# Eight modulation tiles computed in the low-rank stage, three instead of four in each iteration of the mixing

## The reference

```python
mod_all = jnp.einsum('bd,lde->lbe', jax.nn.silu(c), ada_w) + ada_b[:, None, :]
...
shift1, scale1, gate1, shift2, scale2, gate2 = jnp.split(mod_all[i], 6, axis=-1)
h = _modulate(x, shift1, scale1)
...
x = x + gate1[:, None, :] * y
h = _modulate(x, shift2, scale2)
x = x + gate2[:, None, :] * _swiglu(h, f_w1[i], f_w3[i], f_w2[i])
```

## Time and profile before

| | us |
|---|---|
| median of three runs | 2634.53 |
| the profiled execution | 2638.5 |
| span of its trace, from the first to the last instruction | 2636.9 |
| low-rank stage, first matmul to first scan of the mixing | 327.9 to 373.5 |
| mixing, first scan to first matmul of `w_o` | 373.5 to 684.6 |
| steady iteration, scan to scan | 34.5 |

### The profile page before, as it was taken

One profiled execution on the slowest core, in us unless ns is written; L12 is line 12 of the kernel. 1 busy time (PEld: TensorE's weight loads), 2 busy tenths in 40 slices (PEclk: granted clock), 3 DMA queues, 4 the chain that ended last, 5 costly groups with the idle time before them and its releaser, 6 DMA issues.

```text
span 2636.9 us, 53505 instructions
## 1 busy us (share of the span) xinstructions
PE 2526.7 (96%) x20124; PEld 2221.2 (84%) x20124; DVE 1898.7 (72%) x2611; ACT 1251.8 (47%) x1926; POOL 46.3 (2%) x85
## 2 busy tenths in 40 slices
PE   7999997888899999999999999999999999999998
PEld 6888877777788888888888888888888888888887
DVE  6868737988687777777777776687887655555556
ACT  2245555666445444444444554344554444444445
POOL 2000020000000000000000000000000000000000
PEclk9999999999999999999999999999999999999999
DMA  9999864556477888888888768566788666665654
GB/s 400 416 319 306 287 228 153 162 165 211 153 259 255 284 288 287 277 285 289 283 284 271 227 221 286 201 231 229 242 291 284 200 189 190 191 192 187 188 165 138
DMA packets 443401, 640.28 MB, mean 243 GB/s; under 512 B 22048, under 2 KB 403104, under 8 KB 422432
## 3 DMA queue, kind: packets, MB, share of 16 engines
q1 hardware_dynamic: 439552, 626.35, 70.6%
q0 software_dynamic: 3744, 12.59, 1.3%
HBM read 624.18 MB, written 14.68 MB: 242 GB/s over the span
## 4 chain that ended last, share of the span: by engine, by line
PE 67%; DVE 5%; ACT 1%; DMA 1%; issue 1%; DVEq 0%; SPq 0%; ACTq 0%
PE ps L1790 43%; PE ps L1794 22%; DVE ada_ring L1836 1%; DVE wlo L1774 1%; DMA ada_ring<-in_ada 1%; ACT whi L1769 1%; DVE nt L132 0%; PE ps L1425 0%; PE ps L1419 0%; DVE act L145 0%; DVE st L1326 0%; PE ps L1458 0%; DVE lgf L1323 0%; PE ps L1450 0%; PE ps L1440 0%
## 5 line engine op out<-in xcount | busy, mean ns | idle before, releaser
L1774 DVE TENSOR_TENSOR wlo<-raw,whi 128x1024 fp32r<-128x1024 f32 (+1 forms) x736 | 865.3, 1191 | 437.6 <-ACT whi L1769 436.5
L1790 PE MATMUL ps<-act,whi 128*128 128x512 f32 x3528 | 1095.5, 392 | 1.0 <-DVE act L145 1.0
L1769 ACT ACTIVATE whi<-raw 128x1024 fp32r<-128x1024 f32 (+1 forms) x736 | 746.0, 1030 | 638.7 <-PE ps L1794 630.9
L1794 PEld LDWEIGHTS ps<-act,wlo 128*128 128x128 f32 x3528 | 662.6, 188 | 146.3
L1794 PE MATMUL ps<-act,wlo 128*128 128x256 f32 x3528 | 696.3, 279 | 0.0
L1790 PE MATMUL ps<-hid,whi 128*128 128x512 f32 x2176 | 685.6, 396 | 8.1 <-DVE wlo L1774 7.0
L1790 PEld LDWEIGHTS ps<-act,whi 128*128 128x128 f32 x3528 | 534.6, 188 | 1.6 <-DVE wlo L1774 1.0
L1794 PEld LDWEIGHTS ps<-hid,wlo 128*128 128x128 f32 x2176 | 411.5, 189 | 92.6
L1794 PE MATMUL ps<-hid,wlo 128*128 128x256 f32 x2176 | 433.2, 279 | 0.0
L1790 PEld LDWEIGHTS ps<-hid,whi 128*128 128x128 f32 x2176 | 330.9, 189 | 10.7 <-DVE wlo L1774 4.4
L1836 DVE SCALAR_TENSOR_TENSOR ada_ring<-ada_ring,silu 128x2048 f32<-128x2048 f32 x128 | 292.4, 2285 | 12.7 <-DMA ada_ring<-in_ada 12.7
(11 more groups left out here) (273 smaller groups left out, 2062.5 us busy)
## 6 DMA issues: line engine op xcount, KB each, us to landing
raw<-in_f_w SPq DMA_DIRECT2D x480, 512.0 KB, 4.6
ada_ring<-in_ada SPq DMA_DIRECT2D x144, 1024.0 KB, 7.6
raw<-in_a_w_rkv SPq DMA_DIRECT2D x96, 512.0 KB, 7.7
ada_ring<-in_ada SPq DMA_DIRECT2D x64, 512.0 KB, 4.5
raw<-in_b_w_in SPq DMA_DIRECT2D x56, 512.0 KB, 4.2
raw<-in_f_w SPq DMA_DIRECT2D x64, 384.0 KB, 3.9
first_ring<-in_ada SPq DMA_DIRECT2D x16, 1024.0 KB, 12.7
raw<-in_a_w_o SPq DMA_DIRECT2D x32, 512.0 KB, 7.5
```

Of the source, the lines that this page charges most:

```text
L1769: self.nc.scalar.activation(self.whi[:, u % SPL, 0:n], self.raw[:, u, 0:n], ACT.Copy).then_inc(self.s("hi_ready"), 1)
L1774: self.nc.vector.tensor_tensor(self.wlo[:, u % SPL, 0:n], self.raw[:, u, 0:n], self.whi[:, u % SPL, 0:n].bitcast(F32), SUB).then_inc(self. ...
L1790: self.nc.tensor.matmul(self.ps[0:c1 - c0, banks[b], :], hi[:, kk, c0:c1], src[:, k].rearrange("p a t -> p (a t)"), start=k == 0, stop=False)
L1794: last = self.nc.tensor.matmul(self.ps[0:c1 - c0, banks[b], T:2 * T], lo[:, kk, c0:c1], src[:, k, 0, :], start=False, stop=k == ktotal - 1)
```

## The change

Tiles 48 to 55 are computed in the low-rank stage, in a ring of three places of a whole tile (`lora_ring`), in memory that is not used in that stage. The mixing does the other 24 tiles: three in each iteration, six halves, in three of the four places of `ada_ring`.

```diff
-ADA_FIRST = 48
+ADA_LORA, ADA_FIRST = 48, 56
...
     def sync(self, sp):                      # class Loras
         p, s = self.p, self.p.s
+        sp.wait_ge(s("unit_used"), self.units)
+
+        def rows(n):
+            if n > 2:
+                sp.wait_ge(s("ada_added"), ADA_LORA + n - 2)
+            sp.dma_start(p.lora_ring[n % 3][:], p.ada_rows(ADA_LORA + n)).then_inc(s(f"lora_rows{n % 3}"), 16)
+        for n in range(3):
+            rows(n)
         for u in range(RAW):
             sp.wait_ge(s("native_used"), self.n0 + u + 1)
             p.load_unit(sp, u, self.outer(u))
+            if 2 <= u <= 6:
+                rows(u + 1)
...
     def vector(self, dve):                   # class Loras
         for k in range(KT):
-            self.mixed.dve_one(dve, 4, self.p.lmix[1], k, k, k)
+            self.mixed.dve_one(dve, 4, p.lmix[1], k, k, k)
+        for n in range(ADA_FIRST - ADA_LORA):
+            dve.wait_ge(s(f"lora_rows{n % 3}"), 16 * (n // 3 + 1))
+            tile = p.lora_ring[n % 3][:]
+            p.nc.vector.scalar_tensor_tensor(tile, tile, 1.0, p.silu[:], MUL, MUL,
+                                             accum_out=p.mod[:, ADA_LORA + n:ADA_LORA + n + 1]).then_inc(s("ada_added"), 1)
+        at = slice(ADA_LORA, ADA_FIRST)
+        dve.wait_ge(s("ada_added"), ADA_FIRST)
+        p.nc.vector.tensor_tensor(p.mod[:, at], p.mod[:, at], p.pv[:, PV_ADA + ADA_LORA:PV_ADA + ADA_FIRST], ADD).then_inc(s("lora_mods"), 1)
...
-        TILES = 2 * KT // L
+        TILES = (2 * KT - (ADA_FIRST - ADA_LORA)) // L
...
         def place(n):
-            return self.ada_ring[:, n // 2 % 2, (n % 2) * W:(n % 2 + 1) * W]
+            m = n % 3
+            return self.ada_ring[:, m // 2, (m % 2) * W:(m % 2 + 1) * W]
...
-                    if not (isinstance(i, int) and i == 0 and n < 4):
-                        sp.wait_ge(s("ada_half"), i * HALVES + (n - 3))
+                    if not (isinstance(i, int) and i == 0 and n < 3):
+                        sp.wait_ge(s("ada_half"), i * HALVES + (n - 2))
...
             def body(i, more):
-                ada(i, 6, 7)
-                ada(i + 1, 0, 1, 2, 3)
+                ada(i, 4, 5)
+                ada(i + 1, 0, 1, 2)
                 if more:
                     tiles(i + 2)
                 gates(i)
-                ada(i + 1, 4, 5)
+                ada(i + 1, 3)
...
-            ada(0, 0, 1, 2, 3)
+            ada(0, 0, 1, 2)
             tiles(1)
             loras.gates_stored(sp)
-            ada(0, 4, 5)
+            ada(0, 3)
...
-            ada(L - 1, 6, 7)
+            ada(L - 1, 4, 5)
             gates(L - 1)
...
-                adas(i, 5, 6)
+                adas(i, 5)
                 grow(i, "W32", 1, SUB, "P4")
                 if prep:
                     prep_c(i + 1, 1 - q)
-                adas(i, 7)
                 grow(i, "W64", 3, SUB, "W32")
```

More of the change, by code:

```diff
@@ L796, in vector @@
     def vector(self, dve):
-        dve.wait_ge(self.p.s("unit_used"), self.units)
+        p, s = self.p, self.p.s
+        dve.wait_ge(s("unit_used"), self.units)
         for k in range(KT):
-            self.mixed.dve_one(dve, 4, self.p.lmix[1], k, k, k)
+            self.mixed.dve_one(dve, 4, p.lmix[1], k, k, k)
[7 more added lines that the diff above has]
+        p.nc.vector.tensor_tensor(p.mod[:, at], p.mod[:, at], p.pv[:, PV_ADA + ADA_LORA:PV_ADA + ADA_FIRST], ADD).then_inc(s("lora_mods"), 1)
     def pool(self, pool):
@@ L1698, in layout @@
                 b[n] = rw(f"{n}{j}", [P, NC, 2, HD])
+            if j == 0:
+                self.lora_ring = [v("lora_ring0", [P, D], o[0])]
+            else:
+                self.lora_ring += [v(f"lora_ring{n}", [P, D], o_u + 4 * D * (n - 3)) for n in (1, 2)]
             b["bon"] = [rw(f"bon{q}_{j}", [P, T]) for q in range(2)]
@@ L1954, in place @@
         def place(n):
-            return self.ada_ring[:, n // 2 % 2, (n % 2) * W:(n % 2 + 1) * W]
+            m = n % 3
+            return self.ada_ring[:, m // 2, (m % 2) * W:(m % 2 + 1) * W]
         def ada_half(dve, i, n):
-            dve.wait_ge(s(f"half_loaded{n % 4}"), i * 32 + 16 * (n // 4 + 1))
+            dve.wait_ge(s(f"half_loaded{n % 3}"), i * 32 + 16 * (n // 3 + 1))
             nc.vector.scalar_tensor_tensor(place(n), place(n), 1.0, self.silu[:, (n % 2) * W:(n % 2 + 1) * W], MUL, MUL,
@@ L1968, in ada @@
                 for n in ns:
-                    if not (isinstance(i, int) and i == 0 and n < 4):
-                        sp.wait_ge(s("ada_half"), i * HALVES + (n - 3))
+                    if not (isinstance(i, int) and i == 0 and n < 3):
+                        sp.wait_ge(s("ada_half"), i * HALVES + (n - 2))
                     sp.dma_start(place(n), view[bass.ds(i * TILES + (ADA_FIRST + n // 2), 1), :, (n % 2) * W:(n % 2 + 1) * W]
-                                 .rearrange("a p k -> p (a k)")).then_inc(s(f"half_loaded{n % 4}"), 16)
+                                 .rearrange("a p k -> p (a k)")).then_inc(s(f"half_loaded{n % 3}"), 16)
             def projected(i, j):
@@ L2309, in ada_sums @@
             def ada_sums(i):
-                parts = self.parts[:].rearrange("p (m h) -> p m h", h=2)
+                parts = self.parts[:, 0:HALVES].rearrange("p (m h) -> p m h", h=2)
                 dve.wait_ge(s("ada_half"), i * HALVES + HALVES)
@@ L2385, in vector @@
             for u in range(2):
-                dve.sem_inc(s(f"ada_loaded{u}"), 8 * L * TILES)
+                dve.sem_inc(s(f"ada_loaded{u}"), 8 * (L * TILES + (ADA_FIRST - ADA_LORA)))
             at(dve, L - 1, "Yp", 0)
@@ L2659, in build @@
         local = self.mixing_only | {"first_rows_stored", "rows_stored", "gate_stored", "lora_in", "lora_out",
-                                    "lora_taken", "native_used"} | set(ENTRY_ONLY)
+                                    "lora_taken", "native_used", "lora_mods", "lora_rows0", "lora_rows1", "lora_rows2"} | set(ENTRY_ONLY)
         self.nc.clear_and_free_semaphores([self.sems.pop(n) for n in sorted(local)])
```

## The result

The changed kernel took 2640.55 us (median of 20 runs, 2635.72 to 2646.81) beside 2635.55 us of the kernel before (20 runs, 2632.09 to 2639.42). The ratio is 1.0017, with a 95% interval of 1.0011 to 1.0023: slower by some 4.5 us. The prediction was 2634.6 us in a range of 2631 to 2639, so the time lies outside the range, by 1.6 us. The ratio is still within the 0.2% that I called no change.

The account below looks back on a forecast made before the run. DVE, busy 90% of the mixing's iteration, looked like the pacesetter, but the removed halves were judged covered. Profiled 2638.5 us plus 1.0 delay less 0.9 gain gave 2638.6; runs' median 4.0 lower, so 2634.6, range 2631 to 2639.

Parts of the forecast that it names:

- The products, 18.3 us under cover: Low-rank stage: eight products on DVE, 18.3 us, end by 364 to 366, before the scan, and cost nothing.
- my estimate of 2.3 us for a product with two inputs from SBUF: Low-rank stage: by the skill, a late DVE product could hold POOL's first store up to 2.3 us; forecast took 0.
- The backlog, 1.7 MB at 357: Low-rank stage's queues: some 1.7 MB of added tile loads still to be moved at 357 us.
- The delay of the stores and of the scan, 1.0 us of at most 4.2: End of low-rank stage: backlog delays POOL's stores and the scan by 0 to 4.2 us, taken as 1.0.
- What goes out of the mixing, 0.01 us an iteration: Mixing: removing two halves of 1.215 us gains 0.01 us an iteration ahead of W32 and 0 ahead of W64.
- The 0.79 us of the last iteration: Last mixing iteration: DVE is late for W32 and holds PE, so the removal gains 0.79 us.
- The ring of three, 0: Mixing: loading each half when the third before it has been used costs 0, since halves land in time.
- a wait of DVE for a half as a sign of being wrong: Mixing: the forecast is wrong if DVE waits there for a half to arrive.
- the transfers of the low-rank stage collide: Rival, 7%: low-rank loads queued ahead of stores, tiles landing in 12.7 us, mixing begins 5.6 us late, 2640 us.
- DVE sets the pace: Rival, 5%: in the mixing each half taken out counts, gaining 19.4 us, 2615 us.
- PE's code comes late: Rival, 2%: with DMA nearly full, PE's instruction loading leaves a 4.5 us gap in the low-rank stage, 2639 us.

Follow-up runs that it names:

- e3: Changed kernel with only the first three tiles loaded in the low-rank stage, all eight products still made: 2635.70 us, ratio 0.9997 to the kernel before.
- e9: Kernel before, all eight halves kept in the mixing, one half ahead of P2 instead of two, later halves reordered: 2629.12 us, ratio 0.9975.
- e6: Changed kernel with its six halves at other places, none ahead of P2: 2627.05 us, ratio 0.9966 to the kernel before.
- e1: Kernel before with the eight loads and products added to its low-rank stage, mixing still doing all 32 tiles: 2641.85 us, ratio 1.0021.
- e2: Changed kernel without the low-rank stage's tile loads and products, the eight columns set to zero: 2635.62 us, ratio 1.0000 to the kernel before.
- e12: The changed kernel unaltered, executed once more for a second profile: 2637.35 us.
- e4: Changed kernel with five tile places in the low-rank stage, five loads issued at the start and three behind: 2641.97 us, ratio 1.0024 to the kernel before.
- e13: Changed kernel with PE doing six instead of four gate products ahead of the first iteration's sums: 2637.43 us (11 runs), ratio 1.0005 to the kernel before.
- e10: Changed kernel with no half ahead of P2 and without the low-rank stage's tile loads and products: 2621.15 us, ratio 0.9947 to the kernel before.

## Why the prediction was wrong by its own steps

**The products, 18.3 us under cover: right.** They took 2.29 us each and ended at 364.8, forecast 364 to 366. e3 shows that they cost nothing by themselves. DVE beside POOL's issues cost nothing that shows either: the two stores issued from 359.08, beside a product, took 1.45 us together, as they did before. What I had weighed against this from the Trainium skill ("SBUF — State Buffer", section "SBUF: two separate sides") did not show here. That section tells of starved descriptors for a DVE instruction in a two-port mode, so my estimate of 2.3 us for a product with two inputs from SBUF may have gone further than it does.

**The backlog, 1.7 MB at 357: right in size.** It was 1.7 MB. Two parts of the sum made up for each other, which is luck: I had the queues move 400 GB/s from 343 on, and they moved 355 from 341 on, 5.7 MB until 357 in place of 5.5.

**The delay of the stores and of the scan, 1.0 us of at most 4.2: this step failed. It was 4.7 us.** I wrote "Since 2.75 of these 4.2 us are over at 359.75, I take 1.0 us". That lets the backlog drain at the full 400 GB/s, as if nothing else were in the queues. From 357 on the kernel before moves 307 GB/s of its own, so only what is above that drains it, and in the changed kernel the share stayed at 1.03 until 374, four microseconds before the second scan. In the kernel before the queues moved 335 GB/s at a share of 0.98 from 361 to 372, so there was next to no room. The backlog passed whole to the scan: 1.36 us in the stores ahead of the load, and some 3.4 us in its landing, 4.7 us in all. The upper bound of 4.2 us was the value to take, and even this was 0.5 short.

**What a late scan costs: a part that was missing.** I took a microsecond of the scan for a microsecond of the mixing. But PE stood still behind its fourth gate product, 3.25 to 4.98 us in the kernels that load all eight tiles and keep PE's order, and in four of the five such profiles (not in the changed kernel's first) its clock was lower for the work behind it. This, with a scan 0.5 us later still, makes the 3.8 us of the first profile into the 6.4 of the second. It is also a part of why the one profiled pair showed 0.6 us: in the changed kernel's first profile the clock did not fall, and PE's waits for "issue" between M and the second iteration's step of the same kind, which lie elsewhere in each profile, added up to 8.5 us (the longest 3.44) and before to 10.3 (the longest the 4.54 of the earlier trace rows). From the last scan to `w_o` it made up another 2.2 us, more on which below. In all, from the low-rank stage's first matmul to `w_o`'s first the changed kernel took 356.2 us in this pair and the one before 356.7: the pair hides the loss, and only the medians show it.

**What goes out of the mixing, 0.01 us an iteration: right.** The iteration is 34.43 us, and DVE's idle time rose to 1.03 and 1.66 us where I forecast 1.1 and 1.7. What I left out is how much the places ahead of P2 cost: e9 and e6 found 1.1 and 2.1 us an iteration there. The 0.79 us of the last iteration can't be told from these profiles: from the last scan to the first matmul of `w_o` it is 68.2 us in the changed kernel against 70.3 before, but 67.6 in e1, which has all of the halves of before. e2 puts the whole at 0, plus or minus 2.

**The ring of three, 0: right, with a wait that I had excluded.** I had named a wait of DVE for a half as a sign of being wrong. In the last iteration one half was late (in e2 and e12 too, by 1.11 and 1.36 us):

```profile
655.92 1.23 DVE L1984 SCALAR_TENSOR_TENSOR ada_ring<-ada_ring,silu 128x1024 f32<-128x1024 f32 x1 [1.94 <-DMA ada_ring<-in_ada]
...
657.72 0.62 PE L2427 MATMUL ps<-DX 64*64 64x64 f32 x14 [2.56 <-issue]
```

PE stood still for 2.56 us of its own next to it, much as it did for 2.73 us in the kernel before, so the 1.94 us cost nothing that shows.

**The rivals.** The one that happened in its direction is "the transfers of the low-rank stage collide", which I gave 7% and 2640. Its mechanism was half right: the stores and loads behind the backlog, yes; a tile that takes 12.7 us to land, no, since tile 3 landed 5.6 us after its issue. I had made it depend on such slow tiles; the backlog was enough. That its 2640 is what was measured is luck: it counted 5.6 us of delay, of which 1.4 for DVE, where the scan was 4.7 us late and DVE not at all. "DVE sets the pace" at 19.4 us fell with e2. "PE's code comes late" has nothing for it: these waits of PE for "issue" add up to 7.2 to 11.0 us in the profiles that move the 8.4 MB and 6.9 to 10.3 in the others.

**What stays open.** The first iteration holds waits of PE of up to 5.5 us for "issue" that fall in other places in each profile, and no run here tells what they are. How often the clock falls is known from profiles alone, and so its share of the 4.5 us is too. What makes e4 later than the changed kernel was not found. A kernel that joins e6's places with e13's order or with six tiles in the low-rank stage and two elsewhere wasn't tried; as an estimate by the sum of the parts, it would be near e10's 2621.

## What to carry to other kernels

Room in a stage's queues is a number of bytes, up to the moment at which something there is on the critical path: what the queues can move until then, less what they move already. Here 6.3 MB more were free, and of 8.4 MB the 1.7 that were left over made the consumer late by the whole time that they take, though e4 issued them earlier. The price of a late arrival is read at the engine that has to stand still for it, with the clock that it may lose by it; and work taken from a busy engine gave back only what stood ahead of an operation for which others waited, so moving it can be worth more than removing it: moving one half of eight (e9) gained 0.25%, removing two (e2) nothing.

## What the runs showed of the hardware

- The share of the DMA engines and their rate are not the same thing. e4 moved 316 GB/s from 341 to 357 at a share of 1.02, and the changed kernel 401 GB/s from 359 to 368 at 1.04. I had taken 400 GB/s as the rate of full queues; in the stretch with w2, a2, g2 and tiles together it was lower in e4.
- After a wait of PE of 3.25 us (changed) the granted clock stayed at 1.00; after 3.31 (e6), 3.77 (e12), 3.81 (e1) and 4.98 us (e4) the stretch from 378 to 392 had a mean of 0.76. The first of the sums took 1.11 to 1.12 us at the lower level and 0.65 at the upper.
